# Page table loads on another queue, a new order in the opening, and one group of products at a later place: a hybrid decoder step on one core

## The reference

```python
h = RMSNorm(x) * gain                        # 1024 + 32 rows
qa, ka, va, qb, kc, vc, ks, vs, kw, vw, gates = split(h @ w_in)     # 1024 x 2840
# mixer A: dilated window attention; mixer B: three branches on its own keys and values:
#   compressed blocks of 64 tokens, the 16 blocks of best score (selected), a sliding window of 512
# the caches of compressed and selected branches are paged: rows = pool[page_table[b, pos // 128], pos % 128]
# every logit gets a relative-position bias from a table of 32 buckets per head
x = x + concat(mixer_A, gate * branches_of_B) @ w_out
x = x + (silu(conv(g)) * conv(v)) @ w_down,   g, v = split(RMSNorm(x) @ w_up)
y = RMSNorm(x)                               # and all new cache rows are outputs
```

## Time and profile before

| | us |
|---|---|
| median of 3 runs (lowest, highest) | 2107.55 (2105.12, 2110.82) |
| the profiled execution | 2107.46 |
| its span, first to last instruction | 2105.6 |
| PE busy in the span | 2030.3 (96%) |
| DVE, ACT, POOL busy | 1117.3, 521.3, 575.8 |

### The profile page before, as it was taken

The page is one execution under the profiler, slowest core; times in us unless marked ns, Lnnn a source line. Parts: engine busy times, 40 slices in busy tenths (PEclk is TensorE's granted clock), DMA queues, the critical chain, the costliest instruction groups (busy, mean ns, idle before and its releaser), DMA issues. The chain is left out here.

```text
span 2105.6 us, 31735 instructions
## 1 busy us (share of the span) xinstructions
PE 2030.3 (96%) x12334; PEld 1326.6 (63%) x12334; DVE 1117.3 (53%) x2524; ACT 521.3 (25%) x1140; POOL 575.8 (27%) x746
## 2 busy tenths in 40 slices
PE   6999999999987989999999999999999999999998
PEld 3445456666555656667676448888888888634443
DVE  5034455511535555777775467777777756511452
ACT  4111011101323445766675021111111111000001
POOL 0444234202034651112233342222332222304110
PEclk9999999999999999999999999999999999999999
DMA  8467677663697995233152215666666422601101
GB/s 220 142 212 285 245 281 282 247 223 119 230 380 282 421 419 199 101 91 87 53 174 72 81 70 190 207 229 215 209 220 220 141 81 62 240 4 30 43 40 40
DMA packets 156392, 373.04 MB, mean 177 GB/s; under 512 B 36981, under 2 KB 95085, under 8 KB 138189
## 3 DMA queue, kind: packets, MB, share of 16 engines
q1 hardware_dynamic: 126420, 149.63, 22.6%
q0 software_dynamic: 25280, 149.44, 18.2%
q10 hardware_dynamic: 4544, 71.95, 9.7%
HBM read 343.68 MB, written 98.60 MB: 210 GB/s over the span
## 5 line engine op out<-in xcount | busy, mean ns | idle before, releaser
L2947 PE MATMUL ff_ps<-ff_hx,whole_aw 128*128 128x264 f32 x2464 | 550.5, 386 | 0.8 <-DVE ff_hx L3343 0.8
L2947 PEld LDWEIGHTS ff_ps<-ff_hx,whole_aw 128*128 128x128 f32 x2464 | 467.1, 190 | 80.6 <-issue 1.2
L828 DVE STREAM_TRANSPOSE whole_space<-whole_space 128x512 f32<-128x512 f32 x256 | 155.3, 677 | 153.4 <-PE late_bank L637 141.7
L601 PE MATMUL late_bank<-in_w,in_xT 128*128 128x512 f32 (+1 forms) x512 | 201.5, 547 | 0.0
L1195 DVE CUSTOM_DVE_ANT_0 pa_L<-late_bank,whole_space 128x512 f32<-128x512 f32 (+3 forms) x288 | 141.0, 532 | 43.4 <-PE late_bank L1041 41.3
L601 PEld LDWEIGHTS late_bank<-in_w,in_xT 128*128 128x128 f32 x512 | 95.0, 190 | 94.2 <-issue 87.6
L1167 ACT ACTIVATE pa_L<-pa_L,pa_nm 128x640 f32<-128x640 f32 (+3 forms) x192 | 142.0, 741 | 46.4 <-DVE pa_nm L1207 46.1
L2973 PE MATMUL ff_ps<-ff_hx,whole_space 128*128 128x512 f32 x336 | 148.0, 593 | 0.0
L726 ACT ACTIVATE in_yout<-late_bank 128x128 f32<-128x128 f32 (+5 forms) x88 | 40.8, 479 | 378.9 <-PE late_bank L601 199.6
L3427 DVE SCALAR_TENSOR_TENSOR whole_space<-whole_space,ff_kept 128x1024 f32<-128x1024 f32 x88 | 125.3, 1424 | 3.1
L637 PE MATMUL late_bank<-whole_space 128*64 128x256 f32 (+1 forms) x1152 | 121.6, 364 | 0.0
(11 more groups left out here) (436 smaller groups left out, 2669.4 us busy)
## 6 DMA issues: line engine op xcount, KB each, us to landing
out_new_a_k_s<-in_cache_a_k ACTq DMA_DIRECT2D x8, 4088.0 KB
out_new_a_v_s<-in_cache_a_v ACTq DMA_DIRECT2D x8, 4088.0 KB
whole_aw<-in_w_up SPq DMA_DIRECT2D x44, 512.0 KB, 7.2
in_w<-in_w_in SPq DMA_DIRECT2D x5, 2048.0 KB, 11.6
whole_space<-in_cache_a_k SPq DMA_DIRECT2D x8, 1024.0 KB
whole_space<-in_cache_a_v SPq DMA_DIRECT2D x8, 1024.0 KB
ff_hx<-in_w_down SPq DMA_DIRECT2D x14, 512.0 KB, 4.8
whole_space<-in_x_prompt SPq DMA_DIRECT2D x12, 512.0 KB, 9.7
```

The costliest lines, as they stand in the source:

```text
L601: mm = pe.matmul(ps[0:n, b, 0:width], xT[:, k, t * P:t * P + n], w[:, at % WBUF, k, 0:width], start=(k == 0), stop=(k == KC - 1))
L828: last = dve.transpose(put[:, dh, :, k * HD:k * HD + HD].rearrange("p t (g b) -> p t g b", g=2), got[:, :, :, dh, :])
L2947: mm = pe.matmul(ps[:, bank_of(x, j, g), 0:H2], aw[:, j % 2, at, k, :], hx[:, bt, k, g * H2:g * H2 + H2], start=(k == 0), stop=(k == KH - 1))
```

## The change

Five edits in the opening of `front`, one in `sample_selected`:

1. The issues of `far_bias`, `odd`, `ptrc` and `ptr` go from ACT's stream to POOL's, behind three memsets (one of them new).
2. ACT takes a root of a constant that POOL sets, before the first square, so that the root's activation table is loaded there.
3. ACT's squares of the groups 1 and 2 go one or two at a time between copies; the first copy follows root 0.
4. DVE's scalings of the groups 1 and 2 go one at a time between copies.
5. Every wait for POOL's memsets counts two instead of one.
6. `window_values` goes on PE from (b = 0, c = 3) to (b = 1, c = 1), behind `scores(1, 0)`; on DVE its output goes from (0, 3) to (1, 2), behind the copies of the probabilities of sample 0; on POOL `values(1, 0)` goes from b = 2, c = 0 to c = 1, so that the key gather and the bias of (2, 1) come ahead of it.

```diff
 # ACT
-            act.dma_start(far_bias[:, :], ...).then_inc(s_fb, 16)
-            act.dma_start(odd[:, :], io["c_odd"][:, :]).then_inc(s_pg, 16)
-            for d in range(2):
-                act.dma_start(ptrc[d:32:2, :], bass.AP(io["page_table"].tensor, 0, [[1, 16], [16, 4 * NB], [1, 1]]),
-                              allow_slow_non_contiguous=True).then_inc(s_pg, 16)
-            for d in range(2):
-                act.dma_start(ptr[d:P:2, :], bass.AP(io["page_table"].tensor, 0, [[1, NPAGE], [NPAGE, NB], [1, 1]]),
-                              allow_slow_non_contiguous=True).then_inc(s_pg, 16)
...
-            act.wait_ge(s_one, 1)
+            act.wait_ge(s_one, 2)
+            nc.scalar.activation(bias[:, 0:1], bias[:, 0:1], ACT.Sqrt)
             squares(0)
+            squares(1)
+            squares(2)
             root(0)
-            squares(1)
...
+            moved(0)
+            squares(3)
+            squares(4)
+            moved(2)
+            squares(5)
+            moved(4)
+            root(1)
+            for j in (6, 8, 10):
+                moved(j)
+            squares(6)
+            moved(12)
+            squares(7)
+            squares(8)
+            moved(14)
+            root(2)
+            for j in range(16, NX, 2):
+                moved(j)
 # DVE
-            for j in (x for x in range(NX) if not on_act[x]):
-                for g in range(NG):
-                    if before < first_x[g] <= j:
-                        norm(g)
-                before = j
-                copy_out(dve, j, ...).then_inc(s_ev[1], 1)
+            mean_square(0)
+            for t in range(3):
+                scaled(t)
+            moved(1)
+            moved(3)
+            mean_square(1)
+            for t in range(3, 6):
+                moved(2 * t - 1)
+                scaled(t)
+            moved(11)
+            moved(13)
+            mean_square(2)
+            for t in range(6, 9):
+                moved(2 * t + 3)
+                scaled(t)
+            for j in range(21, NX, 2):
+                moved(j)
             indices()
 # POOL
+            pool.memset(bias[:, 0:1], 1.0).then_inc(s_one, 1)
             pool.memset(ss[:, :], 1.0).then_inc(s_one, 1)
             pool.memset(w2, 0.0).then_inc(s_wz, 1)
+            pool.dma_start(far_bias[:, :], ...).then_inc(s_fb, 16)
+            pool.dma_start(odd[:, :], io["c_odd"][:, :]).then_inc(s_pg, 16)
+            for d in range(2):
+                pool.dma_start(ptrc[d:32:2, :], ...).then_inc(s_pg, 16)
+            for d in range(2):
+                pool.dma_start(ptr[d:P:2, :], ...).then_inc(s_pg, 16)
             pool.wait_ge(s_pe, NX)
 # sample_selected: POOL, PE, DVE
-                    if b >= 2:
+                    if b == 2 and c == 1:
+                        values(1, 0)
+                    if b >= 2 and (b, c) != (2, 0):
                         values(b - 1, c)
...
-                    if b == 0 and c == 3:
+                    if b == 1 and c == 1:
                         window_values()
...
-                    if b == 0 and c == 3:
+                    if b >= 1 and c == 2:
+                        prob_copies(dve, False, dve.tensor_copy, b - 1)
+                    if b == 1 and c == 2:
                         for w in range(2):
                             dve.wait_ge(s_we, w + 1)
...
-                    if b >= 1 and c == 2:
-                        prob_copies(dve, False, dve.tensor_copy, b - 1)
```

More of the change, by code:

```diff
@@ L759, in gelu, with moved @@
                 last.then_inc(s_g, 1)
-            act.wait_ge(s_one, 1)
+            def moved(j):
+                copy_out(act, j, copy).then_inc(s_ev[0], 1)
+            act.wait_ge(s_one, 2)
+            nc.scalar.activation(bias[:, 0:1], bias[:, 0:1], ACT.Sqrt)
             squares(0)
+            squares(1)
+            squares(2)
             root(0)
-            squares(1)
-            before = -2
-            for what, n in order:
-                if what == "job" and on_act[n]:
-                    if before < first_x[1] <= n:
-                        root(1)
-                        squares(2)
-                    if before < first_x[2] <= n:
-                        root(2)
-                    before = n
-                    copy_out(act, n, copy).then_inc(s_ev[0], 1)
+            moved(0)
[15 more added lines that the diff above has]
+                moved(j)
+            for what, n in order:
+                if what == "job" and on_act[n] and n >= NX:
+                    moved(n)
                 elif what == "half":
@@ L781, in _, with mean_square @@
         def _(dve):
-            def norm(g):
+            def mean_square(g):
                 c = slice(3 * g, 3 * g + 3)
@@ L845, in out_copy @@
                 last.then_inc(s_o, 1)
[L847 to L854 removed]
+            dve.wait_ge(s_one, 2)
+            mean_square(0)
[15 more added lines that the diff above has]
+                moved(j)
             indices()
```

40 lines of the change are left out of this document (21 added, 19 removed).

## The result

The changed kernel takes **2093.9 us** (median of 9 runs, 2091.35 to 2101.75) against 2109.0 for the kernel before, measured beside it (2103.16 to 2116.69). The ratio is 0.9941, with a 95% interval from 0.9920 to 0.9961: 12.4 us less, between 8 and 17.

What follows compares the result with a forecast made beforehand. The prediction took PE to set the time, with free time in the opening and in waits of the sample stage. Gains of 9.5 (opening) and 7.5 (products) sum to 17.0: 2107.46 to 2090.5 us, range 2085 to 2099.

Steps and rivals of the forecast that it cites:

- What bounds the kernel, and that a gain is kept: Whole kernel: PE sets the time and is 100% busy from 50 us, so an earlier start carries through.
- Rival (1): Sample stage: DMA bound, takes the second gain back; 2098 us if all of it is lost; chance 0.12.
- Rival (3): DVE's `indices`, then PE's fold job: page loads land after 42.4 us, each us costs one; 2102 or slower; chance 0.04.
- Opening, 9.5 predicted: Opening of `front`: copies end at 38.0 us instead of 47.55, a gain of 9.5, from 7 to 11.
- The table jobs' start: Opening, PE: table jobs still start at 8.96 us, as their load keeps its place in ACT's queue.
- What is next late is DVE: Opening: DVE has 22.2 us of work without a gap from 14.2, ending at 36.4 at best.
- The price of an element: Page loads on GpSimd: 4.7 to 7.5 ns a row, 2.4 to 3.8 us for 512, 10 to 17 for all.
- The term for PE's clock: Opening: some table and transpose groups run slow, PE ending at 40.6 instead of 34.8; 38.0 taken for the copies' end.
- The page's sentence on transposes: Opening, PE: the full clock does not engage for transposes; then PE's all-slow sum, ending at 46.4 us, would hold.
- The page table loads leave ACT, one table load goes: Opening, ACT: freed early, squares end at 13.3, first scaling at 14.2, PE goes to transposes at 17.7 instead of 21.63.
- Products, 7.5 predicted: Sample stage: products behind (1,0)'s scores, 0 to 3 us wait for its keys; gain 7.5, from 5 to 9.
- the first of them ends between 641 and 644: Sample stage: the first of five gathers in flight, for chunk (1,0)'s keys, ends then, so PE waits 0 to 3 us.

Runs made afterwards that it cites:

- both parts alone: Two runs against the kernel before: the five opening edits only, 2100.9 us, ratio 0.9960; the later place of the sliding value products only, 2101.15 us, ratio 0.9962.
- held or on ACT's queue: Changed kernel with GpSimd's six loads issued only after table operand and three x tiles arrive, 2091.76 us; or with them back on ACT, 2091.24 us (one execution).
- The products alone: Kernel before with only the sliding value products moved later, its opening untouched: 2101.15 us, ratio 0.9962.
- The swap: Changed kernel with GpSimd's key gathers of (1,0), (1,1) and value gathers of (0,2), (0,3) exchanged: median 2095.22 us, ratio 0.9937 to the kernel before.
- held and swapped: Changed kernel with page loads issued after table operand and first x tiles arrive, and key and value gathers exchanged: 2088.63 us, ratio 0.9890 to the kernel before.

## Why the prediction was right, and where it was off

**What bounds the kernel, and that a gain is kept:** right. PE has no idle time from 50 to 250 us in either kernel, 7.55 of the opening's 8.6 arrive in the sample stage, and both parts alone are faster. Rival (1) did not come: behind the first wait those for keys were 6.2 us against 9.3, and the lead of 12.05 at (1,2)'s keys was 11.8 at the end of the stage. Rival (3) did not come: DVE asks for the page table at 38.6 and does not wait.

**Opening, 9.5 predicted, 8.6 measured (in five executions 5.9 to 9.0).** Three steps were off.

(a) The table jobs' start ("8.96, waits for a load whose place in ACT's queue is unchanged"): the place was, the start was not. It came at 10.12 (9.6 to 11.0 in five executions), and as PE had no gap of note from there to the last transposes, the opening ended that much later. The cause is the small loads on GpSimd's queue, which left the other loads 263 GB/s where ACT's left 383; held or on ACT's queue they let the table jobs start at 8.72 to 9.01. "The rows of x share the engines with these loads in either kernel" is true and hides that they pay more on one queue than on the other. x was late beside these loads too (11.39 to 12.50 where 10 was taken, 9.72 to 10.06 with them held) and cost nothing in this execution, as the prediction said of a late x: the first tile was scaled at 16.9, and PE's table jobs ended at 18.8.

(b) "What is next late is DVE" failed; PE sets the end. Busy times from the start of the table jobs to the weight products, columns as in the earlier trace rows, first of the kernel before, then of the changed one:

```profile
10.20:39.00 28.80, 22.66 (x70) 11.06 (x69) 15.29 (x21) 18.51 (x33) 0.00 (x0) 0.88 1.10 283
```

```profile
10.20:39.00 28.80, 28.32 (x98) 13.97 (x98) 21.04 (x32) 18.74 (x37) 0.31 (x1) 0.94 1.07 300
```

PE went from 22.66 to 28.32 of 28.80 us. DVE was near but not the bound: from its first scaling at 15.66 to 38.6 it waited 2.3 us in all, 0.83 of them for PE's last transposes, where "DVE without gaps from 14 to 37" was a sign named. (The sum for DVE leaves out a copy: fifteen of the 31 jobs are odd, so by its own prices the 36.4 should be 37.1; the work took 20.6 us, less than its 22.2.)

(c) The price of an element was bounded at 2.4 to 3.8 us a load; it was 0.65 to 0.7.

The term for PE's clock, 38.0 taken where all fast gave 34.8, held in size: 3.2 us against some 2.8 here, an estimate from two groups of transposes (5.75 us where 4.94 was counted, 4.50 where half of "about 5" was). But no later table group was slow (3.72 and 3.60), and which stretches are slow changes from execution to execution: the transposes of group 2 took 2.57 us in one and 4.66 in another, so that the size held was in part luck. The page's sentence on transposes that the prediction weighed, the Trainium skill's in "TensorE: Matmul & The Clock Gate", section "Part 4: PE-mode transpose", does not hold here: 24 transposes in 2.57 us are the full clock.

Where the gain was put was also off. The text began with "The page table loads leave ACT, one table load goes"; by the runs the gain needs the order of copies, squares and scalings (without it the full product is at 50.36), the early root gives some 2 us of the first scaling, and the loads' move 0.7 there, against 0.6 to 2.0 us of delay for the table operand. That the order would give all of it alone was not run.

**Products, 7.5 predicted, 4.5 measured.** The mechanism was right, the wait for (1,0)'s keys mis-sized: 0 to 3 us predicted, 3.4 to 4.4 in seven executions with the gathers' old order, and the half clock behind it cost 1.67 + 0.53 = 2.2 (3.67 and 1.59 us against 2.00 and 1.06) where 1 was allowed. The step that failed is not "the first of them ends between 641 and 644" (in the kernel before 15 of the 16 completions of that gather are on record by 643.6) but what was made of it: that end was held against PE's arrival as if both moved forward alike. GpSimd issued the gather only 5.1 us earlier (623.09, 628.21 before) while PE came 7.55 earlier. The queue's first gather follows a line of PE that ran at half clock just then (L1594, 5.43 us for 117 products, 3.88 in the kernel before), where PE's lead was 5.1; from there PE alone gained, as the kernel before lost 4.0 us from 616 to 627. The products alone, with PE 2.4 us earlier, waited 3.83, so the wait does not need the opening. The swap took this wait away and returned the missing part. (1,2)'s keys came 15.6 us after PE ran out, just outside the 11 to 15 named as a sign.

**The sum.** 17.0 predicted; 12.05 in the trace at (1,2)'s keys (8.6 of the opening less 1.1 lost on the way, and 4.5), 11.7 at the end, 12.4 by the runs: the low edge of the 12 to 20 that the prediction gave itself. Both terms were taken too large, so nothing cancelled. The spread between executions is as large: over 62 runs of the kernel before, the span was 2113.9 us on average at a mean granted clock of 0.985 (5 runs) and 2103.0 at 0.990 (4 runs). This is why the parts alone, 8.4 (4 to 13) and 8.0 (4 to 12) by their ratios, do not have to add to 12.4 (8 to 17), and why the swap, for one, is shown by its trace and not by its median.

What stays open: what decides which stretches of the opening run slow; whether held and swapped is faster than the changed kernel in more than the one set of runs that shows it; what the order alone and the early root alone are worth; and why small loads from GpSimd's queue cost the other loads more.

## What to carry to other kernels

A queue that is read from top to bottom hides which of its items matter: before crediting an edit, ask what would still be waited for if it alone were undone; here nothing was left of the gain without the order of copies, and the loads were next to nothing. A queue that is free is not for that reason cheap: the same small loads slowed their neighbours from GpSimd's queue and not from ACT's; hold them until the loads that the start waits for are there. When two engines are near each other in a sum, ask the trace which one waits for the other at the end. When work moves ahead of a wait, look in the issuing queue at what stands ahead of its own operands, for a gather need not move forward by as much as PE does: two gathers whose data then lay unused for 25 us cost 4.25.

## Not expected of the hardware

- A load of 512 four-byte elements held GpSimd 0.65 to 0.7 us; two of them held ACT 5.24 to 6.07 us.
- While such loads were in flight from GpSimd's queue the DMA engines moved 263 GB/s; from ACT's queue, at about the same busy share (1.01 and 1.05), 383.
- A VectorE operation on one column took 5.04 us beside six GpSimd additions in a row, ending with the last; 1.63 at the end of four; 0.16 when they were over.
- One kernel's opening, unchanged, ran its second table group in 3.60 us and in 7.00 us.
